# A two-layer decoder trunk with gathered experts: TensorE's expert product three slots behind the dot, last gathers halved, first weights in more pieces

## The reference

```python
for i in range(DEPTH):                       # DEPTH = 2
    hn = rmsnorm(h, norm_mix[i])
    if i % 3 == 0: y = diff_attention(hn, ...)       # layer 0: w_qkv, two softmaxes, their difference, w_o
    elif i % 3 == 1: y = short_conv(hn, ...)         # layer 1: w_in, gate, width-3 causal conv, w_out
    h = h + y
    h = h + peer_ffn(rmsnorm(h, norm_ffn[i]), ...)

# peer_ffn, per token: 8 heads, each takes the 16 best of 16384 experts by product keys
idx, gates = top16(...)                              # 8 * 16 = 128 experts of each token
act = einsum('chkd,cd->chk', u_tab[idx], xb)
out = einsum('chk,chkd->cd', gelu(act) * gates, v_tab[idx])
```

## Time and profile before

| | |
|---|---|
| median of 3 runs | 1543.71 us (1543.04 to 1544.45) |
| the profiled execution | 1543.85 us, span 1541.7 us, 2.15 us around it |
| busy | PE 88%, DVE 65%, ACT 39%, POOL 38% of the span |
| HBM | 622 MB read, 404 GB/s over the span |
| chain that ended last | DMA 43%, PE 35%, DVE 11%, ACT 7%, issue 3% |
| mean granted TensorE clock | 0.986 of full |

### The profile page before, as it was taken

One profiled execution on the slowest core, in us unless ns is written; L12 is line 12 of the kernel. 1 busy time (PEld: TensorE's weight loads), 2 busy tenths in 40 slices (PEclk: granted clock), 3 DMA queues, 4 the chain that ended last, 5 costly groups with the idle time before them and its releaser, 6 DMA issues.

```text
span 1541.7 us, 12630 instructions
## 1 busy us (share of the span) xinstructions
PE 1352.9 (88%) x3294; PEld 574.4 (37%) x3294; DVE 1005.3 (65%) x2481; ACT 595.9 (39%) x1805; POOL 587.5 (38%) x516
## 2 busy tenths in 40 slices
PE   8899899899868989889887899898979889778787
PEld 3454344344323433334332334343433333222222
DVE  5677878786567867446478635676657867755454
ACT  1324364544333434334334423243434344343333
POOL 0024243344323434335435433333434444344441
PEclk9999999999999999999999999999999999999999
DMA  9659999999999999999999999999999999999996
GB/s 394 247 215 421 421 421 422 421 389 421 421 423 421 416 421 421 421 421 422 421 421 418 422 422 421 416 418 421 405 421 366 422 421 421 421 421 421 422 421 289
DMA packets 85319, 623.92 MB, mean 405 GB/s; under 512 B 9472, under 2 KB 9600, under 8 KB 11648
## 3 DMA queue, kind: packets, MB, share of 16 engines
q0 software_dynamic: 73728, 536.90, 84.3%
q1 hardware_dynamic: 9792, 78.91, 12.4%
q10 hardware_dynamic: 1728, 7.31, 1.2%
HBM read 622.04 MB, written 1.05 MB: 404 GB/s over the span
## 4 chain that ended last, share of the span: by engine, by line
DMA 43%; PE 35%; DVE 11%; ACT 7%; issue 3%; POOL 0%; SPq 0%; ACTq 0%; DVEq 0%; POOLq 0%
DMA ring<-in_peer_uv_dram,idx 42%; PE acc L607 23%; PE pp L364 10%; DVE ring L1379 6%; ACT diag L928 1%; ACT L922 1%; ACT weight L924 1%; PE acc L364 1%; DMA ring<-in_w_qkv_dram 1%; ACT L784 1%; PE tt L379 1%; ACT gelu L922 1%; ACT work L747 1%; PE ss L438 0%; DVE row_f L1145 0%
## 5 line engine op out<-in xcount | busy, mean ns | idle before, releaser
L607 PE MATMUL acc<-ring,diag 128*128 128x512 f32 x2048 | 997.4, 613 | 174.2 <-ACT diag L928 169.5
L705 POOL DMA_INDIRECT ring<-in_peer_uv_dram,idx x512 | 587.3, 1147 | 933.5 <-PE acc L607 816.8
L1379 DVE CUSTOM_DVE_ANT_0 ring<-ring,xf 128x1024 f32<-128x1024 f32 x512 | 627.0, 1226 | 461.4 <-DMA ring<-in_peer_uv_dram,idx 451.5
L607 PEld LDWEIGHTS acc<-ring,diag 128*128 128x128 f32 x2048 | 371.5, 192 | 736.0 <-ACT diag L928 389.5
L922 ACT ACTIVATE gelu<-dots 128x1 f32<-128x1 f32 x512 | 103.6, 202 | 804.5 <-DVE dots L1379 804.1
L928 ACT ACTIVATE diag<-const,weight 128x128 f32<-128x128 f32 x512 | 205.5, 401 | 16.7
L924 ACT ACTIVATE weight<-gelu,gates 128x1 f32<-128x1 f32 x512 | 150.8, 295 | 16.6
L364 PE MATMUL pp<-stream,xT 128*128 128x512 f32 x160 | 81.5, 599 | 0.0
L364 PE MATMUL pp<-stream,rows 128*128 128x512 f32 x128 | 66.3, 599 | 0.0
L364 PEld LDWEIGHTS pp<-stream,xT 128*128 128x128 f32 x160 | 30.3, 192 | 37.1 <-issue 37.1
L1379 DVE DVE_READ_ACCUMULATOR2_ANT dots<- 128x1 f32 x512 | 42.3, 83 | 0.0
(11 more groups left out here) (150 smaller groups left out, 742.6 us busy)
## 6 DMA issues: line engine op xcount, KB each, us to landing
stream<-in_peer_w_q_dram SPq DMA_DIRECT2D x18, 1024.0 KB, 9.3
stream<-in_conv_w_in_dram SPq DMA_DIRECT2D x16, 1024.0 KB, 9.7
stream<-in_w_qkv_dram SPq DMA_DIRECT2D x8, 1024.0 KB, 9.4
ring<-in_peer_uv_dram,idx POOLq DMA_INDIRECT x512, 15.3
ring<-in_w_qkv_dram SPq DMA_DIRECT2D x3, 2048.0 KB, 24.6
stream<-in_w_o_dram SPq DMA_DIRECT2D x4, 1024.0 KB, 17.2
kept<-in_peer_w_q_dram SPq DMA_DIRECT2D x2, 2048.0 KB, 11.6
kept<-in_w_qkv_dram SPq DMA_DIRECT2D x1, 2048.0 KB, 36.5
```

The costliest lines, as they stand in the source:

```text
L607: mm = nc.tensor.matmul(acc[half][:, :], diag[:, s % RING, :], row[:, D + half * 512:D + (half + 1) * 512], start=(k == 0), stop=(k == SLO ...
L705: nc.gpsimd.indirect_dma_start(dst, None, uv_dram, bass.IndirectOffsetOnAxis(idx[:, at:at + 1], 0)).then_inc(landed, 16)
L1379: nc.vector.tensor_tensor_reduce(row[:, 0:D], row[:, 0:D], xf[:, s // SLOTS % 2, :], 1.0, 0.0, ALU.mult, ALU.add, dots[:, s % RING:s % RIN ...
```

## The change

1. **Front.** k = 4 to 7 of the first matrix come as two DMAs instead of one, and PE waits for the first at k = 4 and for the other at k = 6. The second matrix comes as two DMAs of 1 MB (`w_second_in`, `w_in[5]`), and PE waits for each where it needs it. ACT issues its load of `h` after the second piece (k = 1), not the first.
2. **Sides.** Most numbers of `AT` are 1 or 2 lower. Of window 1, the output projection of the first half moves from slots 68 to 75 to slots 60 to 68, the additions to `h` from 87 to 88, and `wq2`, `wq3` from 120, 134 to 112, 120. The ranking's start gets a table (`RANK_AT`); those of (0,3) and (3,0) do one step in a slot, that of (3,0) having done two. In windows 2 and 3 the first projection begins when half of its input is there.
3. **Lag.** PE does slot s-3's product before the sides of slot s, not s-2's.
4. **Last slots.** The last three slots are gathered in halves: three u halves, then three v halves, by indices into a table of half rows that DVE makes with two small operations. PE waits for the v half of each.

```diff
+SPLIT = 3
@@ table AT, numbers from the slot that begins the window before it
-         norm0=45, norm1=77, gain=54, y0=49, y1=81, out00=68, out10=72, out01=84, out11=88, h0=87, f0=89, h1=91, f1=93, scale=92,
-         wq0=93, wq1=104, wq2=120, wq3=134),
-    dict(x=3, in2=8, in4=16, in3=24, in5=32, in0=40, in1=48, z0=25, z1=41, turn_z0=27, turn_z1=43, turn_g0=51, turn_g1=59,
+         norm0=44, norm1=76, gain=54, y0=48, y1=80, out00=60, out10=65, out01=82, out11=86, h0=88, f0=90, h1=91, f1=93, scale=92,
+         wq0=93, wq1=104, wq2=112, wq3=120),
+    dict(x=2, in2=6, in4=14, in3=22, in5=30, in0=38, in1=46, z0=23, z1=39, turn_z0=25, turn_z1=41, turn_g0=49, turn_g1=57,
-LATE_RANK_PROJECT = {1: 0, 2: 25, 3: 50}
+LATE_RANK_PROJECT = {1: 0, 2: 24, 3: 49}
+RANK_AT = {(0, 3): 66, (1, 2): 133, (1, 3): 149}
-RANK_PIECES = {(0, 1): 2, (0, 2): 2, (0, 3): 1, (1, 0): 2, (3, 0): 2}
-LATE_IN_PROJECT = {2: 9, 1: 17, 5: 33, 3: 41}
+RANK_PIECES = {(0, 1): 2, (0, 2): 2, (0, 3): 1, (1, 0): 2}
+LATE_IN_PROJECT = {2: 8, 1: 16, 5: 32, 3: 40}
...
@@ PE, front and slots
                     if k == 4:
                         pe.wait_ge(x_scaled, 2)
+                        pe.wait_ge(w_first_in[3], 16)
+                    if k == 6:
                         pe.wait_ge(w_in[4], 16)
...
                 pe.wait_ge(diag_ready, s + 1)
+                if s >= ALL - SPLIT:
+                    pe.wait_ge(v_last_in[s - ALL], 16)
...
             for s in range(ALL):
-                if s > 1:
-                    add_expert(s - 2)
+                if s > 2:
+                    add_expert(s - 3)
                 along(sides, s)
+            add_expert(ALL - 3)
             add_expert(ALL - 2)
@@ SP
-                sp.dma_start(place[:, 4 * CHUNK:], columns[:, 4 * CHUNK:]).then_inc(w_in[4], 16)
+                sp.dma_start(place[:, 4 * CHUNK:6 * CHUNK], columns[:, 4 * CHUNK:6 * CHUNK]).then_inc(w_first_in[3], 16)
+                sp.dma_start(place[:, 6 * CHUNK:], columns[:, 6 * CHUNK:]).then_inc(w_in[4], 16)
+                place, columns = places[held(0, "in", 2)[0]], matrix_of(0, "in", 2)
+                sp.dma_start(place[:, 0:4 * CHUNK], columns[:, 0:4 * CHUNK]).then_inc(w_second_in, 16)
+                sp.dma_start(place[:, 4 * CHUNK:], columns[:, 4 * CHUNK:]).then_inc(w_in[5], 16)
@@ POOL
-                    nc.gpsimd.indirect_dma_start(dst, None, uv_dram, bass.IndirectOffsetOnAxis(idx[:, at:at + 1], 0)).then_inc(landed, 16)
+                    if s < ALL - SPLIT:
+                        nc.gpsimd.indirect_dma_start(dst, None, uv_dram, bass.IndirectOffsetOnAxis(idx[:, at:at + 1], 0)).then_inc(landed, 16)
+                    else:
+                        last = s - ALL + SPLIT
+                        nc.gpsimd.indirect_dma_start(dst[:, 0:D], None, half_dram, bass.IndirectOffsetOnAxis(idx_last[:, 0, last:last + 1], 0)).then_inc(landed, 16)
+            for s in range(ALL - SPLIT, ALL):
+                dst, _, _ = slot(s)
+                last = s - ALL + SPLIT
+                nc.gpsimd.indirect_dma_start(dst[:, D:], None, half_dram, bass.IndirectOffsetOnAxis(idx_last[:, 1, last:last + 1], 0)).then_inc(v_last_in[s - ALL], 16)
@@ ACT
-                act.wait_ge(w_first_in[0], 16)
+                act.wait_ge(w_first_in[1], 16)
                 act.dma_start(h[:, 0, :], x_rows[0]).then_inc(x_in[0], 16)
```

More of the change, by code:

```diff
@@ L197, in build @@
         gates = sb("gates", [P, 2 * SLOTS])
+        idx_last = sb("idx_last", [P, 2, SPLIT], U32)
         stat = sb("stat", [P, 8])
@@ L230, in build @@
         w_in = {place: sem(f"w_in{place}") for place in range(2, 10)}
-        w_first_in = [sem(f"w_first_in{i}") for i in range(3)]
+        w_first_in = [sem(f"w_first_in{i}") for i in range(4)]
+        w_second_in = sem("w_second_in")
         warm_ready = sem("warm_ready")
@@ L256, in build @@
         uv_in = [sem(f"uv_in{i}") for i in range(RING)]
+        v_last_in = [sem(f"v_last_in{i}") for i in range(SPLIT)]
         dot_done = sem("dot_done")
@@ L350, in wait_weights @@
                         pe.wait_ge(part_in[k // DEEP], 16 * (before + 1))
+                elif (n, what, c) == (0, "in", 2):
+                    if k == 0:
+                        pe.wait_ge(w_second_in, 16)
+                    elif k == HALF:
+                        pe.wait_ge(w_in[place], 16)
                 elif k == 0:
@@ L580, in gated_input @@
                 for i, c in enumerate(in_order(n)):
-                    yield at[f"in{c}"]
-                    if i == 0:
-                        copied(pe, tt, (n, "x", 0), (n, "x", 1))
-                    yield from project(pp, n, "in", c, xTm, at[f"in{c}"])
+                    for half in range(2):
+                        yield at[f"in{c}"] + HALF * half
+                        if i == 0:
+                            copied(pe, tt, (n, "x", half))
+                        yield from project(pp, n, "in", c, xTm, at[f"in{c}"] + HALF * half, range(HALF * half, HALF * (half + 1)))
             def turn_gated(n):
@@ L663, in _ @@
                     load_stream(n, what, c, held(n, what, c)[1], previous.get(place))
-                elif (n, what, c) != (0, "in", 0):
+                elif (n, what, c) not in ((0, "in", 0), (0, "in", 2)):
                     if place in previous:
@@ L844, in late @@
             def late(c):
-                yield from rank(0, c, LATE_RANK_PROJECT[c], LATE_RANK_PROJECT[c] + 13)
+                yield from rank(0, c, LATE_RANK_PROJECT[c])
             def late_input(c):
@@ L890, in experts @@
             def experts(n, c):
-                at = steady_of(n)[f"wq{c}"]
-                yield from rank(n, c, at, at + 13)
+                yield from rank(n, c, steady_of(n)[f"wq{c}"])
             def gated_input(n):
@@ L1152, in ranked @@
                                              float(n // 2 * EXPERTS), None, ALU.add))
+                if (n, c) == (WINDOWS - 1, 3):
+                    for half in range(2):
+                        link(nc.vector.tensor_scalar(idx_last[:, half, :], idx_f[:, 1, TOPK - SPLIT:TOPK], 2.0, float(2 * (n // 2) * EXPERTS + half),
+                                                     ALU.mult, ALU.add))
                 dve.sem_inc(idx_ready, j1 - j0)
```

43 lines of the change are left out of this document (26 added, 17 removed).

## The result

The changed kernel takes **1546.64 us** (median of 20 runs, 1543.41 to 1551.11); the kernel before, run beside it, 1543.51 us (20 runs, 1542.18 to 1545.22). The ratio is 1.0021 with a 95% interval of 1.0015 to 1.0027: slower by 3.1 us, which is outside the forecast's own range (1540.0 to 1542.9) and outside the wider one of 1539.0 to 1545.0. Its runs also lie wider apart, over 7.7 us against 3.0. The profiled execution of after took 1545.4 us, 1.2 less than its median, so the trace shows 1.6 of the 3.1 us.

A forecast was written before the change was run, and what follows sets the result against it. Bound by bytes of gathers and weights; 1543.85 + 0.2 (front) - 1.3 (slots) - 1.2 (last slots) = 1541.55 us profiled, so a median of 1541.4 us. Own range 1540.0 to 1542.9, wider range 1539.0 to 1545.0.

The forecast's parts named there:

- What bounds the kernel: From about 100 us on, the bytes of gathers and weights bound the kernel; PE is close behind but not the bound.
- The front: Before the first gather: PE's saved waits are lost again before the transpose, smaller pieces cost +0.2 us, bounds 0 and +0.9.
- The slots: Main stretch of gathers: lag only shifts sides, new table removes most of the 300 us stall; -1.3 us, ends -7.9 and 0.
- the slower rival: Slots: ring places come free one slot later, fewer gathers under way; some 50 slots make +5.8 us, 1548.5 us; 11%.
- Gathers around 306 to 331 us landing after 12 us or more: Sign the forecast is right, in the stalled stretch: longer time from issue to landing, with GB/s near 415 in that slice.
- The last slots: After the last landings: halved gathers hide dot and ACT behind the v parts; -1.2 us, ends -0.9 and -1.5.
- The clock in the new gap: Front, PE's gap before the transpose at 31.63 us: granted clock falls, adding 1.7 to 3.4 us; 22%.
- The shorter front: Before the first gather: up to 2.7 us of PE's saved waits reach that gather, giving 1538.7 us; 12%.
- Fixed cost at the end: Last gathers: 1.98 us of issue stands open for each of three more DMAs, +5.9 us, 1547.3 us; 3%.
- The change does what it says: Denies a 2% rival: lag moves nothing, pieces arrive no sooner, only the end gains, 1542.6 us.

## Why the prediction was wrong, point by point

**What bounds the kernel**: right. Landings end the dots' waits before and after, and PE's 57.5 us fewer of waiting move nothing.

**The front**, +0.2: right about the pieces. No wait at k = 4, the third projection ends at 29.1 (I said 28.5), the transpose comes after a gap of 2.58 us (about 2.5), and the chain still runs through the whole second matrix. The first gather's 97.07 is just outside the 96.5 give or take 0.5, by a landing that varies by chance. What I left to a rival, the clock, happens in part of the executions and goes with most of what the front costs. So this term was mis-sized: +0.2 us, with bounds of 0 and 0.9, against +1.9 by the ratio of the front alone, with 1.4 us either way.

**The slots**, -1.3, measured +2.1 in the trace: this term failed, and in it this step: "PE's lag of three only shifts PE's sides by one slot against the products: a product still starts when its diagonal is there". PE works in order. With a lag of two, the product behind a side that waits for ACT or DVE belongs to a slot that is one younger, whose diagonal is less often there; with three it is an older one, whose diagonal is ready. In the place shown the product starts 4.3 us after it, its ring place comes free late, and the queue runs short. I had this chain as the slower rival at 11%, and had put against it that "the products' times do not move", which is the wrong step once more. Its size was too large: I priced 5.8 us from 50 slots, and the lag costs 3.5 us (1.0021 against 0.9998), of which the early stretch's bytes are 2.35. Its picture was off as well. I let the rate sink with the time from issue to landing, over 50 slots; in the trace it is full again at a median of 10.1 us, and the loss is a hole of ten microseconds. A place that comes free one slot late everywhere, which is what I wrote, costs 1.5 us in the kernel before.

The other half of the term, that the new table takes away the stall at 300 us, was right for the stall (393 to 419 GB/s) and wrong for the sum: the work moved is still done, and DVE is late 40 us further on (421 to 388). What is left is 0.9994, -0.9 us, not to be told from nothing. "Gathers around 306 to 331 us landing after 12 us or more" did not come. The answer for them, after, to be read against the earlier trace rows:

```profile
DMA to landing us min/median/max: 7.3/9.5/10.7
```

As shallow as before, and yet the stretch moves more bytes. I read the win off one stall and did not ask what the moved steps collide with.

**The last slots**, -1.2: right. The trace gives 1.3, the part alone 1.3. The Trainium skill's fixed part of about 2.0 us for each such DMA (*DMA: Bandwidth & Descriptors*, "Anatomy of one DMA — SWDGE (gpsimd) path") does not show here: the halves land 1.26 us apart, so in a full queue it is hidden. The last addition comes 3.1 us after the last v half, within the 3.0 to 3.5 that I gave.

**The rivals.** The clock in the new gap (22%): real but partial, some executions only, 1.4 to 1.7 us where it fell, at or under the lower end of my 1.7 to 3.4. That the clock would fall in the slots too I had nowhere. The shorter front (12%): did not come. Fixed cost at the end: no. The change does what it says.

**The sum as it turned out**, by ratios: the lag +3.5 us, the table -0.9, the end -1.5, the front +1.9, together +3.0 of 3.1. That this comes out is a weaker test than it looks: the lag's part is the whole change less the change without it, so what is tested is only that the other three, -0.5 us by themselves, are -0.3 together. The lag's part comes out alike from a second pair, free of the falls of the clock in the front: the changed kernel with both gaps filled (1.0002) against the table and last gathers with theirs filled (0.9979), 3.6 us; the pair also differs by the filled front, which measured 0.9997 alone. Yet each part carries 1.4 us either way, so how the 3.1 splits stays open within that. Open too is why the changed kernel's runs scatter; their mean clock does not follow their time. The four kernels with both the new table and a lag of three in the early windows range over 6.0 to 8.1 us, all other experiments over 2.2 to 4.6.

## What to carry to other kernels

A product that waits for nothing must not stand behind one that may wait: before moving an in-order engine's work by a slot, look for the sides that wait on another engine, and count what stands ready behind them. An engine's shorter waits are worth nothing by themselves if it is not the bound, but a buffer it frees later is worth something, and the sign to read is the time from issue to landing: it tells how much reserve the queue has before the rate falls. Two edits that cure the same stall do not add up: time each alone and with the other's taken out, and look at the stretch right behind the cured one.

## What the runs showed of the hardware

A queue of 1 MB indirect gathers keeps 421 GB/s with landings 11.5 to 14.2 us after issue and 420 with 11.3 us (the changed kernel without the lag), and it moved 422 GB/s over 35 us in which they landed 8.0 to 15.6 us after issue. The rate fell to 322 GB/s over the 10 us in which three gathers in a row landed after 7.5 to 7.7 us. The median alone does not tell the rate: around 306 to 331 us it was 9.4 before and 9.5 after, and the rates of 305 to 345 us were 389 and 414. A gather of half the bytes takes half the time in a full queue, 1.26 us against 2.485.

TensorE's granted clock fell from 2.4 towards 1.2 GHz in three executions and stayed up in three others, after the same gap of 2.58 us behind the same work; in the front it cost PE 1.4 to 1.7 us where it fell. Behind the gap at 58 us it was under 1.00 from 60 to 65 us in 12 of the 15 profiled executions that left that gap open and in none of the three that filled it. Two products of zeros kept the clock up behind the gap they filled in all four kernels that had them, and the ratios of all four pairs are lower with them, by 0.08 to 0.19%. A lag of three throughout lowered the mean granted clock, 0.980 against 0.987 in the changed kernel without it.
